# A two-layer decoder: last down weights in quarters, identity products in front of them, first tile in two pairs of blocks

## What is computed

```python
for e in range(N_EXPERTS):                            # 32
    he = jax.nn.silu(xt @ w_gate[e]) * (xt @ w_up[e])   # 1024 -> 512
    out = out + gates[:, e:e + 1] * (he @ w_down[e])    # 512 -> 1024
...
return rms_norm(h, final_norm_w)
```

## Time and profile before

| | |
|---|---|
| Time, median of 3 runs | 1297.04 us (1294.83 to 1299.4) |
| The profiled execution: its time and span | 1296.73 us, 1294.7 us |
| Granted TensorE clock, mean | 0.975 |
| PE busy | 1187.6 us, 92% of the span |
| DVE, ACT busy | 280.0 us, 205.5 us |
| DMA | 463.03 MB, 358 GB/s over the span |

### The profile page before, as it was taken

The page is one execution under the profiler, slowest core; times in us unless marked ns, Lnnn a source line. Parts: engine busy times, 40 slices in busy tenths (PEclk is TensorE's granted clock), DMA queues, the critical chain, the costliest instruction groups (busy, mean ns, idle before and its releaser), DMA issues.

```text
span 1294.7 us, 15031 instructions
## 1 busy us (share of the span) xinstructions
PE 1187.6 (92%) x5996; PEld 584.3 (45%) x5996; DVE 280.0 (22%) x681; ACT 205.5 (16%) x487; POOL 32.4 (3%) x42
## 2 busy tenths in 40 slices
PE   7999999999999999989587999999999999976695
PEld 5874765453444444543232466553444444422231
DVE  5741552141111111100000337241111111100001
ACT  2224332120000000000001335321000000000002
POOL 0001210000000000000000011100000000000000
PEclk9999999999999999998898999999999999998798
DMA  9930159589999999999999762689999999999997
GB/s 357 359 130 26 49 199 426 236 337 426 428 426 426 428 426 425 425 425 425 426 427 415 311 266 92 240 352 426 426 426 426 427 427 425 428 427 427 426 427 279
DMA packets 84728, 463.03 MB, mean 358 GB/s; under 512 B 7552, under 2 KB 9648, under 8 KB 36528
## 3 DMA queue, kind: packets, MB, share of 16 engines
q1 hardware_dynamic: 84656, 462.02, 86.4%
HBM read 460.91 MB, written 1.07 MB: 357 GB/s over the span
## 4 chain that ended last, share of the span: by engine, by line
PE 77%; DMA 11%; SPq 8%; DVE 1%; ACT 1%; issue 1%; DVEq 0%; ACTq 0%
PE bank L1607 21%; PE bank L420 15%; PE bank L1616 12%; SPq L273 8%; PE bank L1574 6%; PE bank L1591 6%; DMA h<-in_w_down 5%; PE bank L403 3%; PE bank L1947 3%; DMA own<-in_w_down 2%; DMA late<-in_w_down 2%; DMA h<-in_w_gate 2%; PE bank L359 2%; PE bank L1638 1%; PE bank L388 1%
## 5 line engine op out<-in xcount | busy, mean ns | idle before, releaser
L1607 PE MATMUL bank<-own,work 128*64 128x512 f32 (+1 forms) x1112 | 262.0, 611 | 21.5 <-DMA own<-in_w_up 11.8
L1607 PE MATMUL bank<-late,work 128*32 128x512 f32 (+1 forms) x568 | 146.7, 615 | 7.8 <-DMA own<-in_w_up 7.8
L1616 PE MATMUL bank<-own,work 128*32 128x512 f32 (+1 forms) x480 | 127.0, 646 | 25.7 <-DMA h<-in_w_down 10.1
L1607 PEld LDWEIGHTS bank<-own,work 128*64 128x64 f32 (+1 forms) x1112 | 75.2, 126 | 147.7 <-issue 147.4
L1475 DVE TENSOR_TENSOR work<-work,bank 128x512 f32<-128x512 f32 x24 | 25.5, 1063 | 467.2 <-ACT work L1538 467.2
L1574 PEld LDWEIGHTS bank<-work,xs 128*128 128x128 f32 x736 | 85.6, 191 | 38.4 <-issue 38.4
L1538 ACT ACTIVATE work<-bank 128x512 f32<-128x512 f32 x24 | 14.3, 597 | 522.5 <-PE bank L1607 522.5
L1574 PE MATMUL bank<-work,xs 128*128 128x128 f32 x736 | 94.4, 281 | 0.0
L1591 PE MATMUL bank<-work 128*128 128x512 f32 x192 | 87.1, 595 | 3.1 <-DVE work L1480 1.6
L420 PE MATMUL bank<-xnT,own 128*128 128x256 f32 x384 | 84.7, 380 | 0.0
L1616 PE MATMUL bank<-late,work 128*64 128x512 f32 (+1 forms) x224 | 71.0, 741 | 9.5 <-DMA own<-in_w_down 4.3
(11 more groups left out here) (327 smaller groups left out, 1293.2 us busy)
## 6 DMA issues: line engine op xcount, KB each, us to landing
own<-in_w_up SPq DMA_DIRECT2D x78, 1024.0 KB, 26.5
own<-in_w_gate SPq DMA_DIRECT2D x61, 1024.0 KB, 26.1
own<-in_w_down SPq DMA_DIRECT2D x56, 1024.0 KB, 26.1
late<-in_w_gate SPq DMA_DIRECT2D x40, 1024.0 KB, 25.8
late<-in_w_up SPq DMA_DIRECT2D x31, 1024.0 KB, 26.8
late<-in_w_down SPq DMA_DIRECT2D x27, 1024.0 KB, 25.9
own<-in_a_in_w SPq DMA_DIRECT2D x17, 1024.0 KB, 13.5
h<-in_w_down SPq DMA_DIRECT2D x10, 1024.0 KB, 29.4
```

What stands on the lines that cost most here:

```text
L1607: ins = pe.matmul(bank[q * T:(q + 1) * T, :], self.xg[:, at:at + T], cut(tile(q), k=4)[:, k, :], start=(half == 0 and k == 0), stop=(half ...
L1616: ins = pe.matmul(self.b_down[out][q * T:(q + 1) * T, :], self.turned[:, at:at + T], cut(tile(q), j=2)[:, j, 512 * out:512 * out + 512], s ...
```

## The change

Four edits:

1. **Quarters.** The second 512 columns of the last unit's four `half` 1 granules come as two quarters of 256 columns, each as four DMAs: all four third quarters first (`third_loaded`), then all four last quarters (`rest_loaded`). PE sums them in two banks, the third quarter in `b_down[1]` and the last one in `b_gather`. It does the third quarter, waits for DVE's copy of it and scatters these 256 columns; then it waits for the last quarter, and does the same. In `half` 0 the same three pieces (512, 256 and 256 columns) are used.
2. **Identity products.** In the last unit two of them stand in front of the wait for `hid` and four behind `turn_hid`, in front of the waits for `turned` and the first down granules. They write `b_gather`.
3. **First tile.** The loop over the four k of the first half of the sum is cut in two pairs: k = 0, 1 for all four output blocks, then k = 2, 3 for all four.
4. Two semaphores of the mixer of layer 0 (`mk_ev`, `mv_ev`) get the names of two that layer 1 has anyway.

Edits 1 and 2 are in both layers, since a layer's last unit has the same code. The diff without the renaming:

```diff
+                    for pair in range(2):
+                        for j in range(4):
+                            for k in (2 * pair, 2 * pair + 1):
+                                if j == 0:
+                                    pe.wait_ge(s["xw_ev"], k + 1)
+                                if j == 0 and k == 2:
+                                    c.wait_job(pe, ("mixer", 0, 0))
+                                pe.matmul(U.bank(("conv", j))[:, 0:256], c.cols_at(0, k)[:, P * j:P * j + P], cut(xTw, k=KD)[:, k, :],
+                                          start=(k == 0), stop=False)
...
             most = self.beyond(sp)
-            for job in jobs:
-                if self.in_two(job):
-                    sp.dma_start(self.column_half(job, 1), self.job_source(job, quad)[:, :, 512:1024]).then_inc(s["rest_loaded"], 16)
+            for at, loaded in ((slice(512, 768), s["third_loaded"]), (slice(768, 1024), s["rest_loaded"])):
+                for job in jobs:
+                    if self.in_pieces(job):
+                        sp.dma_start(self.columns(job, at), self.job_source(job, quad)[:, :, at]).then_inc(loaded, 16)
...
-                dve.wait_ge(s["down_done"], u * 2 + 2)
-                dve.tensor_copy(self.y[1][:, :], self.b_down[1][:, :]).then_inc(s["y1_ready"], 1)
-                if not last:
+                if last:
+                    dve.wait_ge(s["third_down"], 1)
+                    dve.tensor_copy(self.y[1][:, 0:256], self.b_down[1][:, 0:256]).then_inc(s["y1_ready"], 1)
+                    dve.wait_ge(s["down_done"], u * 2 + 2)
+                    dve.tensor_copy(self.y[1][:, 256:512], self.b_gather[:, 256:512]).then_inc(s["y1_ready"], 1)
+                else:
...
+            whole = [(self.b_down[0], 0, 512), (self.b_down[1], 512, 1024)]
+            split = [whole[0], (self.b_down[1], 512, 768), (self.b_gather, 768, 1024)]
+
+            def down(half, T, tile, pieces=whole):
+                for bank, a, b in pieces:
                     for j in range(2):
                         for q in range(P // T):
...
+                if last:
+                    keep_busy(2, self.b_gather)
                 pe.wait_ge(s["hid_ready"], u + 1)
                 turn_hid(s["turned"])
+                if last:
+                    keep_busy(4, self.b_gather)
...
                     else:
-                        down(half, T, tile, (0,)).then_inc(s["out_done"], 1)
+                        down(half, T, tile, pieces[:1]).then_inc(s["out_done"], 1)
                         if last:
                             pe.wait_ge(s["y_ready"], u + 1)
                             pe.wait_ge(s["gates_ready"], u + 1)
                             scatter((0,)).then_inc(s["half_summed"], 1)
+                            pe.wait_ge(s["third_loaded"], 16 * (P // T))
+                            down(half, T, tile, pieces[1:2]).then_inc(s["third_down"], 1)
+                            pe.wait_ge(s["y1_ready"], u + 1)
+                            scatter((1,), at=slice(0, 256))
                             pe.wait_ge(s["rest_loaded"], 16 * (P // T))
-                        down(half, T, tile, (1,)).then_inc(s["down_done"], 1)
+                        down(half, T, tile, pieces[-1:]).then_inc(s["down_done"], 1)
...
-                pe.wait_ge(s["y1_ready"], u + 1)
-                scatter((1,), s["scattered"] if last else None)
+                if last:
+                    pe.wait_ge(s["y1_ready"], u + 2)
+                    scatter((1,), s["scattered"], slice(256, 512))
+                else:
+                    pe.wait_ge(s["y1_ready"], u + 1)
+                    scatter((1,))
```

More of the change, by code:

```diff
@@ L1055, in _ @@
                     pe.wait_ge(s["pt_ev"], i + 1)
[L1056 removed]
+                    pe.wait_ge(s["kv_ev"], 2)
                     attend_values(c, pe, out, mv, pTs, i)
@@ L1363, in _ @@
                 sp.wait_ge(*self.released(before(job)))
-                if self.in_two(job):
-                    for_half, src = self.column_half(job, 0), self.job_source(job, quad)
-                    sp.dma_start(for_half, src[:, :, 0:512]).then_inc(c.w_loaded[JOB_AT[job][0]], 16)
+                if self.in_pieces(job):
+                    first = slice(0, 512)
+                    sp.dma_start(self.columns(job, first), self.job_source(job, quad)[:, :, first]).then_inc(c.w_loaded[JOB_AT[job][0]], 16)
                 else:
@@ L1586, in turn_gates, with scatter @@
                 ins.then_inc(signal, 1)
-            def scatter(outs=(0, 1), each=None):
+            def scatter(outs=(0, 1), each=None, at=slice(0, 512)):
                 for out in outs:
                     for t in range(NT):
-                        ins = pe.matmul(self.sums[2 * t + out][:, :], self.gates_T[:, t * P:(t + 1) * P], self.y[out][:, :],
+                        ins = pe.matmul(self.sums[2 * t + out][:, at], self.gates_T[:, t * P:(t + 1) * P], self.y[out][:, at],
                                         start=False, stop=True, skip_group_check=True)
@@ L1609, in gate_up @@
                 return ins
-            def down(half, T, tile, outs=(0, 1)):
-                for out in outs:
+            whole = [(self.b_down[0], 0, 512), (self.b_down[1], 512, 1024)]
+            split = [whole[0], (self.b_down[1], 512, 768), (self.b_gather, 768, 1024)]
+            def down(half, T, tile, pieces=whole):
+                for bank, a, b in pieces:
                     for j in range(2):
@@ L1615, in down, with keep_busy @@
                             at = (2 * half + j) * P + q * T
-                            ins = pe.matmul(self.b_down[out][q * T:(q + 1) * T, :], self.turned[:, at:at + T],
-                                            cut(tile(q), j=2)[:, j, 512 * out:512 * out + 512],
+                            ins = pe.matmul(bank[q * T:(q + 1) * T, a % 512:a % 512 + b - a], self.turned[:, at:at + T],
+                                            cut(tile(q), j=2)[:, j, a:b],
                                             start=(half == 0 and j == 0), stop=(half == 1 and j == 1))
                 return ins
-            def keep_busy(n):
+            def keep_busy(n, bank):
                 for _ in range(n):
-                    pe.matmul(self.b_turn[:, :], c.f("ident"), c.small[:, 0:512], start=True, stop=True)
+                    pe.matmul(bank[:, :], c.f("ident"), c.small[:, 0:512], start=True, stop=True)
             def side(i):
@@ L1675, in unit @@
                     tile = lambda q: c.slot(("expert", layer, u, "down", half, q))
+                    pieces = split if last else whole
                     if half == 0:
-                        down(half, T, tile).then_inc(s["down_done"], 1)
+                        down(half, T, tile, pieces).then_inc(s["down_done"], 1)
                     else:
-                        down(half, T, tile, (0,)).then_inc(s["out_done"], 1)
+                        down(half, T, tile, pieces[:1]).then_inc(s["out_done"], 1)
                         if last:
```

26 lines of the change are left out of this document (14 added, 12 removed).

## The result

The changed kernel takes 1301.84 us (median of 10 runs, 1300.86 to 1303.18), the kernel before on the same chip 1297.18 (10 runs, 1294.83 to 1299.97). The ratio is 1.0031, with a 95% interval of 1.0021 to 1.004: slower by 0.3%, and outside the predicted range. The profiled execution took 1302.64 (span 1300.6), 5.9 more than that of before.

What follows compares the result with a forecast made beforehand. PE was taken to set the time at both layer ends, by 0.6 us, transfers close behind. First tile -0.13, layer 0 -0.35 and layer 1 +0.08 made -0.4, so 1296.6 us, no change; range 1293.2 to 1299.8.

Steps and rivals of the forecast that it cites:

- The step that failed: Both layers: PE and the queue of weights start from what PE has freed, so what is gained early is kept.
- D: Quarters' transfers: small pieces are slow, each quarter takes the 1.3 us of a half; in all 1302.9 us, slower; 5%.
- E: Down products, both layers: the identity products overrun if the clock falls before them; +3.2, 1300.2 us, slower; 4%.
- Quarters: Behind the first scatter: the split lengthens PE's chain, price 0.58 us in layer 0 and 1.11 in layer 1.
- Rival C: Behind the first scatter: a transfer binds and the split saves, -2.1 us in layer 0, -1.6 in layer 1, about 1293; 6%.
- Identity products: Before the down products: clock up for `half` 0, 3.6 us; gain 0.93 us in layer 0, 1.03 in layer 1.
- Layer 1's landing: Layer 1's last unit: first columns land at 1277.19, and halves of 512 KB land 1.3 us each.
- layer 1's last stretch: Layer 1's tail: -1.03 us from the identity products and +1.11 from the split, together +0.08.
- First tile: First tile: pairs remove PE's wait for the second part of the weights; -0.13 us, bounds nothing and 2.4.
- rival B: First tile: the clock rises sooner; gives up to -2.4 + 0.13, so 1294.3 us; 9%.

Runs made afterwards that it cites:

- the best version: The changed kernel with 180 more PE instructions in layer 0 (276 in front of its branch) and no more work: ratio 0.998, 1295.8 us.
- the run with layer 1 moved: The changed kernel with 120 more PE instructions in layer 1's last unit alone: ratio 1.0025, 1301.3 us.
- The other pair: The changed kernel with 120 more PE instructions in layer 0, with the first tile in its old order (0.9997) and in its new order (0.9994).

## Why the prediction was wrong

**The step that failed** is the sentence behind the sum: "PE and the queue of weights in both layers start from what PE has freed, so what is gained early is kept." It wasn't kept. In layer 0 PE comes to the last scatter 1.32 sooner and to `L420` 3.89 later. What stands between is a branch of PE's own queue, which no term of the sum held: the part on the edits counted work and waits of added instructions, never where their code puts the code behind them. In the profiled execution the added instructions cost 6.1 us by their position, 15 times the forecast of the whole change. No rival came near it; the slower ones, D and E, name other places, and neither occurred.

**Quarters: right.** From the start of the first scatter in layer 0 to the end of the last one I had 7.21, and measured 710.35 + 1.13 - 704.14 = 7.34. In layer 1 I had 6.99 from the first scatter to ACT's square, and measured 7.01 (1286.49 to 1293.50). DVE's copies of 256 columns take 0.42 as taken. That the last quarter isn't waited for held too, and with it that the split has little to pay for it. Without the quarters the kernel measures 0.9985, with them, well placed, 0.998: no difference that can be told. Rival C's case, PE waiting for the other columns, needs a late landing; in the kernel without the quarters PE does wait for them in layer 1, 1.57 us, to 1280.64, where the prediction had 0.6 for an unsplit kernel.

**Identity products: right in mechanism, 1.0 per layer as forecast.** `half` 0 takes 3.65 (forecast 3.6). `half` 1 starts 0.14 behind its landing in layer 0 (701.37, 701.51), where it was 1.06 late before. In layer 1 it starts 0.17 behind a landing that is itself late; in the best version, where the landing isn't, 0.12 behind it (1278.26, 1278.38), where it was 1.16 late before. The times are less sure than the traces. Without the stall the kernels with and without these products differ by 0.0017, about 2 us, which is what the two gains of 0.93 and 1.03 add up to, but their intervals overlap (0.997 to 0.9991, 0.9987 to 1.0007). With the stall (1.0031 with, 1.0025 without) the difference has the other sign, and can't be told from none.

**Layer 1's landing: a term mis-sized.** The prediction let the last granule land where the queue's bytes put it. A fetch of 16 KB between two landings made 2.7 of 1.3, and the clock fell in the pause. The waiting and the clock cost 3.0 us against the run with layer 1 moved (1.6 and 1.4). Against the kernel before, layer 1's last stretch cost 2.2 in place of +0.08: 0.4 up to `half` 1, 1.4 of clock, 1.1 of the split, and 0.7 back in the final norm, most of it at the stores that a fetch had held up before. The 1.4 is luck in part: in the two other executions with a late landing PE idled 2.25 and 2.42, and kept the upper level.

**First tile: the term was too small.** I had -0.13, where the run of this edit alone says -1.9 (0.6 to 3.2 by its interval). The other pair, 0.9997 and 0.9994, says -0.4 and can't tell it from nothing, so the size stays open. I read one execution, in which PE began at 8.96. It begins between 7.0 and 9.2 over the profiled executions. The old order then still pauses until the second transfer, at 10.9, and the pace doubles later: with 100 more instructions PE began at 8.14 and came to `L982` 12.6 later, in the new order 9.3 to 10.9 later. In the mean the new order is 1.2 shorter, an estimate from three executions of the old one and ten of the new. So rival B (9%) is partly right, and the answer lies between the term and its bound of -2.4. That the profiled after is 1.89 sooner at `L982` (17.44 against 19.33) is its earlier start alone.

**The sum as it came out**, in the profiled executions: the start -1.9, which is luck; layer 0's gain and split -0.9 + 0.7; branch and clock +6.1; layer 1's tail +2.2. Together +6.2, measured +5.9; between the two tails 0.2 comes back (3.89 late at `L420`, 3.66 at `half` 0).

**What stays open:** where the edges lie; how much of the late landing and of the held-up stores is in an average execution, so that the 4.7 us between the medians aren't split into terms; and what the first tile is worth.

## What to carry to other kernels

When a change adds or removes instructions in front of a branch that is taken, list the branch rows of each engine's queue before and after. A stall of "issue" with no releaser is a sign of it. Compare variants only at positions that both run free, or else an ablation prices the position and not the edit. And a term read from one execution's start carries that execution's luck, so bound it by what a different start would make of it.

## What the runs showed of the hardware that was not expected

- The same taken branch of PE takes 5.86 to 5.96 us or 0.36 to 0.46 in layer 0, and 3.55 to 3.81 or 0.33 to 0.44 in layer 1. Whether it stalls goes by the instructions in front, modulo 256: in layer 0 free at 0, 20, 24, 216 and 252, stalled at 72, 92, 96 and 100. In layer 0 a block is fetched 3.4 to 3.8 us behind the branch in either case. The same branch takes 0.05 to 0.07 on SP, DVE and ACT.
- The instruction that stalls isn't all: in the pause of 4.9 us PE's granted clock falls to 0.50, and the next 16 records of 512 columns take 8.20 instead of 7.03.
- The fetch of one block lands among the data. In layer 1 of the changed kernel it stretched the gap between two landings of 512 KB from 1.3 to 2.7 us. The Trainium skill ("Runtime: NRT & Kernel Launch", Instruction fetch mechanics) calls the cost of crossing a block "mostly hidden"; it wasn't for a fetch that fell into the last transfer that PE waits for.
